# A hybrid decoder step: the last input-projection panel split in three, the state pass in two, and LayerNorms shared out anew

## The reference

```python
def layer_norm(x, g, b):
    mu = jnp.mean(x, -1, keepdims=True)
    var = jnp.mean(jnp.square(x - mu), -1, keepdims=True)
    return (x - mu) * lax.rsqrt(var + LN_EPS) * g + b

def step(s, inp):                        # gated delta rule, one chunk of tokens
    qi, ki, vi, gi, bi = inp
    gcum = jnp.cumsum(gi, -1)
    decay = exp(gcum_i - gcum_j) below the diagonal, else 0
    kb = ki * bi
    lower = strict(kb @ ki.T) * decay
    tmat = inverse(eye + lower)
    u = tmat @ (vi * bi); w = tmat @ (kb * exp(gcum))
    v_new = u - w @ s
    out = (qi * exp(gcum)) @ s + ((qi @ ki.T) * decay) @ v_new
    s = s * exp(g_last) + (ki * exp(g_last - gcum)).T @ v_new

# layer 0: w_in (conv, gates) -> [delta net | attention] -> w_out; layer 1: w_in, gated short convolution, w_out
x = layer_norm(ALPHA * x + mixer(x), ln_mix_g, ln_mix_b)
u, gt = split(x @ w_up); x = layer_norm(ALPHA * x + (gelu(conv3(u)) * gt) @ w_down, ln_ffn_g, ln_ffn_b)
```

## Time and profile before

| | us |
| --- | --- |
| median of three runs | 1192.31 (1190.45 to 1195.57) |
| the profiled execution | 1191.3 |
| its span | 1189.6 |
| TensorE busy | 1093.2 (92% of the span) |
| VectorE busy | 692.3 (58%) |
| ScalarE busy | 557.7 (47%) |
| GpSimd busy | 287.1 (24%) |

### The profile page before, as it was taken

How to read it: one execution, slowest core, us unless ns; L and a number is a source line. 1 busy time by engine, 2 the same in 40 slices (tenths; PEclk the granted TensorE clock), 3 DMA queues, 4 the chain that set the end, 5 groups by cost and what they waited for, 6 DMA issues and landing times.

```text
span 1189.6 us, 19995 instructions
## 1 busy us (share of the span) xinstructions
PE 1093.2 (92%) x6991; PEld 986.7 (83%) x6991; DVE 692.3 (58%) x1190; ACT 557.7 (47%) x882; POOL 287.1 (24%) x271
## 2 busy tenths in 40 slices
PE   6999969876899999897999999979999799999996
PEld 5999868755566666586999999969999699999995
DVE  4843544556776777646666663355564666665344
ACT  3337511245667766536444443354334744444324
POOL 8400123411666767433000000212003300000111
PEclk9989969979999999898999999999999899999998
DMA  7424200175899887542444433434445244444321
GB/s 228 153 99 147 72 0 1 45 234 182 303 303 308 306 294 274 180 164 81 144 144 141 141 141 125 157 119 141 142 142 151 72 141 141 143 155 162 132 86 45
DMA packets 120881, 182.58 MB, mean 153 GB/s; under 512 B 6224, under 2 KB 61615, under 8 KB 120750
## 3 DMA queue, kind: packets, MB, share of 16 engines
q1 hardware_dynamic: 118402, 174.61, 44.1%
q0 software_dynamic: 2416, 7.16, 2.1%
HBM read 176.12 MB, written 5.63 MB: 153 GB/s over the span
## 4 chain that ended last, share of the span: by engine, by line
PE 80%; DVE 10%; ACT 5%; issue 2%; DMA 1%; POOL 1%; SPq 0%; ACTq 0%; DVEq 0%; POOLq 0%
PE bank L1676 74%; PE bank L1974 4%; DVE kTl L1124 2%; ACT hi L725 1%; DVE xres L1124 1%; DMA raw<-w_in_mix 1%; DVE lo L1117 1%; ACT xres L1009 1%; PE bank L2092 0%; POOL xl L676 0%; DVE sbias L1421 0%; DVE gs L1417 0%; DVE sbias L1412 0%; PE bank L2161 0%; ACT kTh L725 0%
## 5 line engine op out<-in xcount | busy, mean ns | idle before, releaser
L1676 PE MATMUL bank<-xh,hi 128*128 128x320 f32 x1184 | 373.5, 315 | 28.7 <-POOL xl L676 24.0
L1676 PE MATMUL bank<-xl,hi 128*128 128x320 f32 x1184 | 371.3, 314 | 0.0
L1676 PE MATMUL bank<-xh,lo 128*128 128x320 f32 x1184 | 370.8, 313 | 0.0
L1117 DVE TENSOR_TENSOR lo<-raw,hi 128x2048 fp32r<-128x2048 f32 x102 | 240.6, 2359 | 191.4 <-ACT hi L725 191.4
L725 ACT ACTIVATE hi<-raw 128x2048 fp32r (+2 forms) x112 | 205.4, 1834 | 112.6 <-PE bank L1676 110.2
L1676 PEld LDWEIGHTS bank<-xh,hi 128*128 128x128 f32 x1184 | 227.3, 192 | 31.6 <-issue 28.4
L1676 PEld LDWEIGHTS bank<-xl,hi 128*128 128x128 f32 x1184 | 227.4, 192 | 0.1
L1676 PEld LDWEIGHTS bank<-xh,lo 128*128 128x128 f32 x1184 | 227.3, 192 | 0.0
L1676 PE MATMUL bank<-hh,hi 128*128 128x320 f32 x416 | 129.3, 311 | 1.3 <-DVE hraw L1124 1.3
L1676 PE MATMUL bank<-hh,lo 128*128 128x320 f32 x416 | 128.4, 309 | 0.0
L1676 PE MATMUL bank<-hl,hi 128*128 128x320 f32 x416 | 128.4, 309 | 0.0
(11 more groups left out here) (394 smaller groups left out, 1541.8 us busy)
## 6 DMA issues: line engine op xcount, KB each, us to landing
raw<-w_up SPq DMA_DIRECT2D x44, 1024.0 KB
kring<-cache_k SPq DMA_DIRECT2D x88, 256.0 KB, 3.6
vring<-cache_v SPq DMA_DIRECT2D x88, 256.0 KB, 4.8
raw<-w_down SPq DMA_DIRECT2D x8, 2048.0 KB
raw<-w_in_mix SPq DMA_DIRECT2D x6, 2048.0 KB
raw<-cache_k SPq DMA_DIRECT2D x40, 256.0 KB, 3.5
raw<-cache_v SPq DMA_DIRECT2D x40, 256.0 KB, 4.9
raw<-w_in_sc SPq DMA_DIRECT2D x8, 1024.0 KB
```

The source lines that it names most:

```text
L1117: dve.tensor_tensor(lo[:, p], weight(n)[:, :, 256 * p:256 * p + 256], hi[:, p], ALU.subtract)\
L1676: return pe.matmul(out, lhsT, rhs, start=start, stop=stop, **kw)
```

## The change

It has two parts. In the delta net the second panel of the last slot is done in three pieces, chunks 0–1, 2–4 and 5–7, which add up in the same banks: one ahead of `cumulative(2)`, one behind `products(2)`, one behind `products(0)`. The state pass is done in two halves of 16 states, in bank 7, the first ahead of `cumulative(1)`, the second behind `products(1)`; its result is copied out after the last tile's decay. Banks and waits follow:

```diff
-        AT = {2: 4, 0: 0, 1: 4}
+        ROWS_AT, GATES_AT = {2: 4, 0: 0, 1: 4}, {2: 6, 0: 6, 1: 2}
...
                 if t == 0:
+                    DV.wait(pe, "L2")
+                    AC.wait(pe, "decay2")
+                if t == 1:
                     pe.wait_ge(s["rel_act"], 32)
-                if t == 1:
-                    DV.wait(pe, "tok2")
-                    AC.wait(pe, "decay2")
...
+            def second_panel(k0, nk):
+                project(6, xh, xl, nk, lambda j: pe.wait_ge(s["rel_act"], 24 + (j + 1)), nothing, k0, k0 == 0, k0 + nk == KD,
+                        (1,), k0, k0 + nk == KD)
...
+            second_panel(0, 2)
             cumulative(2)
             products(2)
-            mix_slot(6, panels=(1,))
+            second_panel(2, 3)
             token_major(2)
             cumulative(0)
             products(0)
+            second_panel(5, 3)
             pe.wait_ge(s["s0_in0"], 64)
             DV.wait(pe, "qg2")
-            for i in range(32):
-                ins = mm(bank[5][:, 16 * i:16 * i + 16], s0[:, i, :], kq[:, 16 * i:16 * i + 16])
-            PE.up(ins, "ksT")
+            DV.wait(pe, "gcl0")
+            state_rows(0)
             cumulative(1)
             token_major(0)
             products(1)
+            PE.up(state_rows(16), "ksT")
             token_major(1)
```

```diff
     "act": """
-sq0_6 sq0_7 msq0 lnv0 rstd0 ln0_0 lnh0_0 ln0_1 lnh0_1 ln0_2 lnh0_2 ln0_3 lnh0_3 ln0_4 lnh0_4 ln0_5 lnh0_5 ln0_6 lnh0_6
+sq0_6 sq0_7 msq0 lnv0 rstd0 lnh0_0 lnh0_1 lnh0_2 lnh0_3 lnh0_4 lnh0_5 lnh0_6 lnh0_7 f0_hist f0_tail0 ...
...
+            def centre(n):
+                DV.wait(pool, f"mean{n}")
+                AC.wait(pool, f"sq{n}_7")
+                for m in (KD - 2, KD - 1):
+                    PO.up(pool.tensor_tensor(xres[:, m, :], xres[:, m, :], lnt[:, 4, :], ALU.subtract), f"centred{n}_{m}")
...
+                for m in POOL_X:
+                    AC.wait(pool, f"lnh{n}_{m}")
+                    shifted(m)
+                    PO.wait(pool, f"xr{n}_{m}")
+                    PO.up(pool.tensor_tensor(xl[:, m, :], xres[:, m, :], xh[:, m, :], ALU.subtract), f"x{n}_{m}")
                 for m in range(KD):
-                    AC.wait(pool, f"lnh{n}_{m}")
-                    PO.up(pool.tensor_tensor(xl[:, m, :], xres[:, m, :], xh[:, m, :], ALU.subtract), f"x{n}_{m}")
+                    if m not in POOL_X:
+                        DV.wait(pool, f"xl{n}_{m}")
+                        shifted(m)
...
                 for m in range(KD):
+                    if m == 6 and following < S_END:
+                        split_hi(following, 1)
                     DV.wait(act, f"t2_{n}_{m}")
-                    AC.up(act.activation(xres[:, m, :], hraw[:, m % 2, :], ACT.Identity, scale=vec(gpack, grow + m),
-                                         bias=vec(bpack, brow + m)), f"ln{n}_{m}")
-                    if n < 3:
-                        AC.wait(act, f"ln{n}_{m}")
-                        AC.up(copy(xh[:, m, :], xres[:, m, :]), f"lnh{n}_{m}")
+                    out, name = (xh, f"lnh{n}_{m}") if n < 3 else (xres, f"ln{n}_{m}")
+                    AC.up(act.activation(out[:, m, :], xres[:, m, :], ACT.Identity, bias=vec(bpack, brow + m)), name)
...
+                def scaled(m):
+                    if m >= KD - 2:
+                        PO.wait(dve, f"centred{n}_{m}")
+                    DV.up(dve.scalar_tensor_tensor(out=xres[:, m, :], in0=xres[:, m, :], scalar=vec(gpack, grow + m),
+                                                   in1=lnt[:, 3, :], op0=ALU.mult, op1=ALU.mult), f"t2_{n}_{m}")
+                def rest(m):
+                    if n < 3 and m not in POOL_X:
+                        DV.wait(dve, f"t2_{n}_{m}")
+                        AC.wait(dve, f"lnh{n}_{m}")
+                        DV.up(dve.scalar_tensor_tensor(out=xl[:, m, :], in0=xres[:, m, :], scalar=vec(bpack, brow + m),
+                                                       in1=xh[:, m, :], op0=ALU.add, op1=ALU.subtract), f"xl{n}_{m}")
...
+                if n:
+                    PO.wait(dve, f"xr{n - 1}_{m}")
```

More of the change, by code:

```diff
@@ L997, in square, with norm @@
                 AC.up(act.activation(sq[:, m % 2, :], xres[:, m, :], ACT.Square), f"sq{n}_{m}")
-            def norm(n, gpack, grow, bpack, brow):
+            def norm(n, gpack, grow, bpack, brow, following):
                 act.preload_act_table(ACT.Ln)
@@ L1082, in _ @@
             down(0, 1)
-            norm(1, 1, PB_LFG, 1, PB_LFB)
+            norm(1, 1, PB_LFG, 1, PB_LFB, S_SC)
             history("sc", KD)
@@ L1100, in _ @@
             out_proj(S_SCO, 2)
[L1101 removed]
+            norm(2, 0, PA_LMG + KD, 0, PA_LMB + KD, S_UP[1])
             history("f1", KF)
@@ L1104, in _ @@
             down(1, 3)
-            norm(3, 1, PB_LFG + KD, 1, PB_LFB + KD)
+            norm(3, 1, PB_LFG + KD, 1, PB_LFB + KD, S_END)
             for i in (1, 3, 5):
@@ L1545, in norm @@
                 DV.up(dve.tensor_scalar(lnt[:, 3, :], lnt[:, 3, :], 0.0, LN_EPS, ALU.max, ALU.add), f"var{n}")
-                for m in range(KD):
-                    ins = tt(xres[:, m, :], xres[:, m, :], lnt[:, 4, :], ALU.subtract)
+                for m in range(1, KD - 2):
+                    ins = centre(m)
                 DV.up(ins, f"centred{n}")
@@ L1550, in norm @@
                 AC.wait(dve, f"rstd{n}")
-                for m in range(KD):
-                    if m >= 2:
-                        AC.wait(dve, f"ln{n}_{m - 2}")
-                    DV.up(tt(hraw[:, m % 2, :], xres[:, m, :], lnt[:, 3, :], ALU.mult), f"t2_{n}_{m}")
+                PE.wait(dve, f"stat{n}")
+                scaled(0)
+                scaled(1)
+                for m in range(2, KD):
+                    scaled(m)
+                    rest(m - 2)
+                rest(KD - 2)
+                rest(KD - 1)
                 if following < S_END:
@@ L1621, in _ @@
             out_proj(S_OUT, 0)
-            norm(0, S_UP[0])
+            norm(0, 0, PA_LMG, 0, PA_LMB, S_UP[0])
             AC.wait(dve, "f0_hist")
@@ L1625, in _ @@
             down(0, 1)
-            norm(1, S_SC)
+            norm(1, 1, PB_LFG, 1, PB_LFB, S_SC)
             AC.wait(dve, "sc_hist")
@@ L1661, in _ @@
             out_proj(S_SCO, 2)
-            norm(2, S_UP[1])
+            norm(2, 0, PA_LMG + KD, 0, PA_LMB + KD, S_UP[1])
             AC.wait(dve, "f1_hist")
@@ L1665, in _ @@
             down(1, 3)
-            norm(3, S_END)
+            norm(3, 1, PB_LFG + KD, 1, PB_LFB + KD, S_END)
             for i in (0, 2, 4):
@@ L2062, in stats, with mean, square, normed_ready @@
             def stats(n):
+                def mean(x, start, stop):
+                    return mm(bank[4][:, 0:TOK], onesD[:, :], x, start, stop)
+                def square(x, start, stop):
+                    return mm(bank[5][:, 0:TOK], onesD[:, :], x, start, stop)
                 PO.wait(pe, f"accs{n}_{KD - 3}")
-                mm(bank[4][:, 0:TOK], onesD[:, :], lnt[:, 0, :], True, False)
-                DV.wait(pe, f"r{n}_7")
-                for m in (KD - 2, KD - 1):
-                    ins = mm(bank[4][:, 0:TOK], onesD[:, :], xres[:, m, :], False, m == KD - 1)
-                PE.up(ins, f"mean{n}")
-                PO.wait(pe, f"accq{n}_{KD - 3}")
-                mm(bank[5][:, 0:TOK], onesD[:, :], lnt[:, 1, :], True, False)
-                AC.wait(pe, f"sq{n}_7")
-                for m in (KD - 2, KD - 1):
-                    ins = mm(bank[5][:, 0:TOK], onesD[:, :], sq[:, m % 2, :], False, m == KD - 1)
-                PE.up(ins, f"stat{n}")
+                mean(lnt[:, 0, :], True, False)
+                PO.wait(pe, f"accq{n}_{KD - 3}")
+                square(lnt[:, 1, :], True, False)
+                DV.wait(pe, f"r{n}_6")
+                mean(xres[:, 6, :], False, False)
+                AC.wait(pe, f"sq{n}_6")
+                square(sq[:, 0, :], False, False)
+                DV.wait(pe, f"r{n}_7")
+                PE.up(mean(xres[:, 7, :], False, True), f"mean{n}")
+                AC.wait(pe, f"sq{n}_7")
+                PE.up(square(sq[:, 1, :], False, True), f"stat{n}")
+            def normed_ready(n, k):
+                if k in POOL_X:
+                    PO.wait(pe, f"x{n}_{k}")
+                else:
+                    DV.wait(pe, f"xl{n}_{k}")
             hist_loads = [1]
```

98 lines of the change are left out of this document (59 added, 39 removed).

## The result

The changed kernel took 1179.31 us (median of four runs, 1176.41 to 1179.5), the kernel before 1191.73 beside it: a ratio of 0.9887, 95% interval 0.9866 to 0.9907. A second series gave 0.9859 (0.9836 to 0.9882), 1176.7 beside 1193.86. The prediction said 1181. The span of the profiled execution is 1177.6 us, 12.0 less.

The account below looks back on a forecast made before the run. The prediction found the chain of waits on TensorE for 80%. From 1191.3 us it took 8.6 for the delta net and 2.6 for the LayerNorms: 1180.1 profiled, 1.0 below the median of the runs, so 1181, range 1176 to 1189.

Parts of the forecast that it names:

- The last tile's chain: Delta net: VectorE's chain for the last tile starts earlier with the state pass halved; `token_major(1)` 8.6 us earlier, at 157.7.
- The two bounds of the prediction: Before `token_major(1)`: VectorE's L of the last tile at 155.8 to 156.7, TensorE's second state half until 157.7.
- The panel's pieces: Delta net: the first piece ahead of `cumulative(2)` lets `token_major(2)` start near 135.6 instead of 140.61.
- What follows moves with it: Behind the delta net: the inversion moves with `token_major(1)`, so its 8.6 us count in full.
- The LayerNorms: Four norms gain 0.2, 1.8, 0.2 and 0.4, in sum 2.6 us; bounds 7.0 gained to 7.1 lost.
- The first matmul of a norm: TensorE's start after the last residual comes 1.7 us earlier; 1.4 of it counted at the second panel.
- The conversion: ScalarE's half-panel conversion ahead of a norm's table load falls from the chain before the first matmul: 1.90 us.
- GpSimd's two differences: In a norm, two subtractions of 0.88 us each on GpSimd push VectorE's by up to 1.76; 1.5 taken.
- GpSimd and VectorE shut each other out: In the norms, whichever of the two engines comes second waits until the other's instruction has ended; `lo` 2.96 us against 2.29 alone.
- rival 1: LayerNorms: GpSimd yields, its shifts slip into VectorE's gaps and the norms keep 7.0 us; 1176.7, chance 0.14.
- Rival 2: Delta net: TensorE's clock falls early, so `token_major(1)` gains only 4.0 us; 1185.7, chance 0.12.
- Rivals 3 and 4: All six shifts ahead of `lo`, 1190.8, chance 0.12; TensorE idles until its clock falls in first feed-forward slot, 1199.5, 0.06.

Follow-up runs that it names:

- state_whole: Changed kernel with the state pass undivided, ahead of `cumulative(1)`; `token_major(1)` came at 163.40 and TensorE idled 5.17 us.
- panel_whole: Changed kernel with the panel undivided between `products(2)` and `token_major(2)`; `token_major(1)` came 30.4 us after the first panel's end, 29.5 and 28.8 in the changed kernel.
- hi_at4: Changed kernel with ScalarE's conversion inside the norm ahead of chunk 4 in place of chunk 6; second slots 25.55, 25.02, 25.56 us after the last residuals.
- shift_late: Changed kernel with GpSimd's six late shifts waiting until the projection's first slot is through; second slots 26.29, 25.66, 26.31 us after the last residuals.

## Why the prediction was right, and where not

The sum came out near, 12.0 for 11.2 in the profiled execution, in part by luck: the delta net gave what was forecast, but the norms gave 3.5 more than counted, and 2.6 were lost in a stretch for which the prediction had nothing.

1. *The last tile's chain is what TensorE waits for; the halves of the state pass bring it forward.* Right, and shown by `state_whole`. `token_major(1)` was predicted at 157.7 and came at 157.82.
2. *How it came to 157.7.* By two errors that cancel. The chain was to start at 147.9 to 148.8 and started at 149.84, as the clock was down in `cumulative(1)` already, a little earlier than assumed. And TensorE's second half was to take 6.6 us and end last; it took 3.64, as the clock was back by then, and VectorE ended last. The two bounds of the prediction lay within 2 us of each other (155.8 to 156.7 and 157.7), so the sum could not be far off; that it agrees to 0.1 us is luck. The sign that the idling would be gone or below 1 us did not come, as 2.66 remained.
3. *The panel's pieces.* The prediction gave them a start of `token_major(2)` at 135.6, and 135.75 was measured. But that place is not on the path that decides: `panel_whole` lost 0 to 1.6 us only.
4. *What follows moves with it.* Not wholly: 2.6 of 8.5 us did not arrive at norm 0 in the profiled execution, and as much in its repeat. In the six other kernels with the same instructions up to there the stretch took 373.0 to 376.2 us, so up to 2.9 of the 8.5 were lost, and in one of them nothing. No step had that, and its cause is open.
5. *The LayerNorms, 2.6 in the sum, measured 6.1.* This is the term that was mis-sized, and the main error is the second slot behind norms 0 and 2. Three shifts in `lo`'s way were to cost VectorE 2.6 us, with 1.45 of slack, and to make the slot 1.2 late, so that 0.2 remained of 1.4. VectorE lost 1.85 us in the convolution (3.85 for 2.00) and 0.3 ahead of it (1.21 for 0.90). But in norm 0 it began this work 19.4 us after the last residual, where it had begun after 21.6: 2.2 earlier, not 1.4. So `lo` ended 26.5 after the residual, as before (26.6), TensorE waited 0.22 for it, and 0.5 in all went from the second panel's gain of 1.9. So 1.4 remained, not 0.2. Norm 1 gave 2.4 for 1.8, norm 3 1.1 for 0.4: there eight passes of ScalarE without a scale went from 4.85 to 3.80, and the sum had no term for that.
6. *The first matmul of a norm.* It came 2.1, 2.7 and 2.1 earlier (1.7 predicted), and of this 1.9, 2.5 and 1.9 were left at the second panel (1.4). In norm 0 two errors cancel in it. The conversion was to give 1.90; the squared mean began only 0.9 earlier (2.7 after the last residual for 3.6), as it now waits 0.92 for the copy of the mean, which came 2.20 after the last residual and in the kernel before 1.44. On the other side GpSimd's two differences were to cost 1.5, more than the 0.6 to 0.9 that the shorter chain gives; VectorE's five took 2.75 us for 2.0, a loss of 0.7, and from the squared mean to the first scaling the norm got 0.5 shorter. The single pass of ScalarE and `xl` on VectorE gave 0.7 (0.6 predicted); no run tests these two alone. The first panel, which was to need its 9.96 us as before, took 10.15 with waits of 1.01 and 0.21 in it, and 9.41 in `hi_at4`, where these waits are nearly gone: its slow start was shorter than counted.
7. *GpSimd and VectorE shut each other out.* Right in the main. The changed kernel's trace shows also what no row of before did: the convolution's four instructions and the shifts take turns one by one, each instruction of VectorE taking about half a microsecond longer. The Trainium skill ("SBUF — State Buffer", section "Who interferes with whom") says that a VectorE instruction with two inputs in SBUF contends with a GpSimd instruction that reads SBUF, over a pair of ports that is locked exclusively. The trace agrees in that each of the four ended about 0.4 us after the shift that it overlaps at its start, and in 3.85 against 2.00. But a turn of one instruction each took 0.94 us, while alone the convolution's follow each other in 0.48 and the shifts in 0.68, which makes 1.16: a part of each runs beside the other. And a loss of VectorE's is not a loss on the chain; that hangs on the slack.

The rivals: the norms came near to rival 1's gain (7.0) without its mechanism, since GpSimd did not yield. Rival 2 did not come: the first half of the state pass ran at 1.00, and the fall to half clock was over after `token_major(0)`. Rivals 3 and 4 did not come, as TensorE never waited long in the first slot.

## What to carry to other kernels

Where a wait ends with another engine's chain, look for work of one's own that stands ahead of that chain's start and is needed only later, and cut it there: half of a 9 us pass was worth 6.6 to 8.2 us, the finer cut of the panel 0 to 1.6. A contention that the trace shows should be priced at the place where someone waits, less the slack there, and not as the sum of what the blocked engine loses. And when work is moved into a chain, try more than one place: moved from ahead of the norm to chunk 6, the same conversion lost 0.5 us over three norms, and to chunk 4 it gained 2.4.

## What the runs showed of the hardware

VectorE and GpSimd instructions that share no data held each other up: the same four instructions took 3.85 us beside GpSimd's shifts and 2.00 without, and a turn of one each took 0.94 us where they need 0.48 and 0.68 alone. Two shifts alone, in `shift_late`:

```profile
564.35 1.40 POOL L684 TENSOR_TENSOR xres<-xres,par 128x320 f32<-128x320 f32 x2
```

In a stretch of some 375 us the time differed by up to 3.2 us between profiles with the same instructions; in its tail the length went with the granted clock, 24.5 us at 0.86 and 27.0 at 0.75. That is more than most of the single edits here are worth. Such edits were read from distances inside the trace, which agree from one profile to the next within 0.05 us up to the second slots of norms 0 to 2, and not from the total. The distance from the last residual to the end is less steady: 17.0 to 17.4 us in profiles in which norm 3 ran alike.
